# Order of the softmax steps and of the rotary products in the latent attention of a diffusion backbone step

## What is computed

```
q_nope, q_rope = mla_queries(...)          # rmsnorm(x @ w_dq) @ w_uq, 8 heads of 128 + 64
q_rope = rope_2d(q_rope)                   # latent tokens only
k_nope = (ckv @ w_uk).reshape(b, nk, 8, 128)
v = (ckv @ w_uv).reshape(b, nk, 8, 128)
s = (einsum('bqhd,bkhd->bhqk', q_nope, k_nope)
     + einsum('bqhr,bkr->bhqk', q_rope, k_rope)) * MLA_SCALE
p = softmax(s, axis=-1)
o = einsum('bhqk,bkhd->bqhd', p, v)
out = o.reshape(b, -1, 1024) @ w_o
```

## Time and profile before

| What | us |
|---|---|
| Median of three runs | 3872.28 |
| Profiled execution | 3875.15 |
| its span on the core | 3873.3 |
| TensorE matmuls, busy in the span | 3490.6 (90%) |
| VectorE busy | 2095.7 (54%) |
| ScalarE busy | 1322.9 (34%) |
| GpSimd busy | 1294.9 (33%) |
| Mean granted clock of TensorE | 0.957 |
| Key products with the four swaps | 3108.22 to 3130.79 |
| Value products | 3130.79 to 3149.6 |
| Loop over the items with the last value product | 3150.3 to 3316.0 |

### The profile page before, as it was taken

The page is one execution under the profiler, slowest core; times in us unless marked ns, Lnnn a source line. Parts: engine busy times, 40 slices in busy tenths (PEclk is TensorE's granted clock), DMA queues, the critical chain, the costliest instruction groups (busy, mean ns, idle before and its releaser), DMA issues.

```text
span 3873.3 us, 67086 instructions
## 1 busy us (share of the span) xinstructions
PE 3490.6 (90%) x24914; PEld 3232.6 (83%) x24914; DVE 2095.7 (54%) x3521; ACT 1322.9 (34%) x2244; POOL 1294.9 (33%) x577
## 2 busy tenths in 40 slices
PE   4899999999999988983699999999998698999998
PEld 2689999898899977962588888889997576789997
DVE  8553674564356558388676766435654554341113
ACT  2253224414422254374233322442224223443223
POOL 0255334545533344302300000553335210454334
PEclk9999999999999999976799999999999799999999
DMA  6434554433454433466121110345443210343223
GB/s 222 137 120 148 189 195 142 120 92 115 131 179 169 149 110 117 134 207 206 51 60 53 54 58 27 123 131 177 166 151 117 63 36 1 93 126 97 74 73 116
DMA packets 173378, 457.72 MB, mean 118 GB/s; under 512 B 56784, under 2 KB 66448, under 8 KB 172432
## 3 DMA queue, kind: packets, MB, share of 16 engines
q1 hardware_dynamic: 145408, 438.46, 35.5%
q10 hardware_dynamic: 27792, 16.83, 1.4%
HBM read 416.79 MB, written 38.44 MB: 118 GB/s over the span
## 4 chain that ended last, share of the span: by engine, by line
issue 73%; POOL 15%; PE 6%; POOLq 2%; DMA 1%; ACT 1%; DVE 1%; DVEq 0%; ACTq 0%; SPq 0%
POOL ws L687 15%; PE banks L760 2%; PE banks L781 1%; PE banks L765 1%; POOLq L723 1%; POOLq L718 1%; PE banks L791 1%; POOLq L695 0%; PE banks L985 0%; PE banks L1015 0%; DMA inv_a<-blk_d 0%; PE banks L1038 0%; DMA wr<-in_w_slabs 0%; POOLq L686 0%; DMA l<-in_l 0%
## 5 line engine op out<-in xcount | busy, mean ns | idle before, releaser
L687 POOL TENSOR_TENSOR ws<-wr,ws 128x1024 fp32r<-128x1024 f32 x509 | 1239.5, 2436 | 2405.6 <-ACT ws L1453 2404.9
L1453 ACT ACTIVATE ws<-wr 128x1024 fp32r<-128x1024 f32 x509 | 538.0, 1057 | 1117.2 <-PE banks L765 441.4
L760 PE MATMUL banks<-hs,ws 128*128 128x320 f32 x3712 | 564.3, 309 | 0.4 <-DVE hs L2496 0.3
L760 PEld LDWEIGHTS banks<-hs,ws 128*128 128x128 f32 x3712 | 549.3, 188 | 1.2 <-DVE hs L2496 0.9
L781 PE MATMUL banks<-hs,ws 128*128 128x320 f32 (+2 forms) x2624 | 443.2, 320 | 58.6 <-DVE hs L2141 19.6
L781 PEld LDWEIGHTS banks<-hs,ws 128*128 128x128 f32 x2624 | 404.0, 194 | 87.4 <-issue 31.7
L781 PE MATMUL banks<-fs,ws 128*128 128x320 f32 x2304 | 374.1, 314 | 20.0 <-DVE acc L2862 11.3
L781 PEld LDWEIGHTS banks<-fs,ws 128*128 128x128 f32 x2304 | 347.2, 190 | 37.8 <-issue 13.8
L2294 DVE SCALAR_TENSOR_TENSOR mjunk<-mr,banks 128x1024 f32<-128x1024 f32 x284 | 335.6, 1219 | 73.6 <-DMA mr<-in_m_slabs 48.5
L760 PE MATMUL banks<-fs,ws 128*128 128x320 f32 x2304 | 351.7, 310 | 0.0
L760 PEld LDWEIGHTS banks<-fs,ws 128*128 128x128 f32 x2304 | 342.3, 189 | 2.4 <-issue 2.4
(11 more groups left out here) (308 smaller groups left out, 4528.1 us busy)
## 6 DMA issues: line engine op xcount, KB each, us to landing
wr<-in_w_slabs SPq DMA_DIRECT2D x509, 512.0 KB, 3.6
mr<-in_m_slabs SPq DMA_DIRECT2D x167, 512.0 KB, 5.0
ar_d<-ar SPq DMA_DIRECT2D x16, 640.0 KB, 4.0
bk_d<-bt SPq DMA_DIRECT2D x16, 640.0 KB, 5.2
ar<-ar_d SPq DMA_DIRECT2D x16, 640.0 KB, 4.2
bk<-bk_d SPq DMA_DIRECT2D x16, 640.0 KB, 5.4
mx<-in_m_slabs SPq DMA_DIRECT2D x16, 512.0 KB, 6.6
rkv<-rkv_d SPq DMA_DIRECT2D x24, 320.0 KB, 4.8
```

The source lines that it names most:

```text
L687: pool.tensor_tensor(ws[s % 2][:, 1, :], wr[:, s % 2, :], ws[s % 2][:, 0, :].bitcast(F32), ALU.subtract).then_inc(lo_ready, 1)
L760: pe.matmul(pu[:, t % 2, h, 0:HT], ws[s % 2][:, 0, k * P:(k + 1) * P], src[:, k, part, h * HT:(h + 1) * HT], start=(k + part == 0), stop=F ...
L1453: act.activation(ws[s % 2][:, 0, :], wr[:, s % 2, :], ACT.Copy).then_inc(hi_ready, 1)
```

## The change

It has two parts. On VectorE the loop over the items now does `maximum(n + 1)` ahead of `normalise(n)` rather than behind it. And the four swaps on TensorE and the four rotations on VectorE, which stood between the key products, now stand together ahead of them. No instruction is added or removed.

```diff
@@ TensorE, latent_attention @@
                         product(j, NQ, j * QR, lambda k: hs[:, k], slab[0])
                     slab[0] += 1
+                for j in range(MH // 2):
+                    swapped(1 + j, qr[:, j, 0:LAT], t_q + MH + j + 1)
                 pe.wait_ge(h_ready, h_tiles[0] + NQ + NKV)
...
                     for j in range(4):
                         product(j, NKV, j * KVR, lambda k: hs[:, NQ + k], s)
-                        if j % 2:
-                            i = 2 * b + j // 2
-                            swapped(1 + i, qr[:, i, 0:LAT], t_q + MH + i + 1)
                     slab[0] += 1
@@ VectorE, latent_attention @@
                     take_tile(qr[:, j, :])
                 dve.drain()
+                for j in range(MH // 2):
+                    rotate(1 + j, qr[:, j, 0:LAT])
                 for b in range(2):
...
                     for j in range(4):
                         take_tile(kn[:, 4 * b + j, 0:T])
-                        if j % 2:
-                            i = 2 * b + j // 2
-                            rotate(1 + i, qr[:, i, 0:LAT])
...
                 for n in range(n_items):
-                    normalise(n)
                     if n + 1 < n_items:
                         maximum(n + 1)
+                    normalise(n)
                     if n % 5 == 1 and n > 5:
                         take_values(n // 5 - 1)
```

## The result

The changed kernel takes 3990.22 us (median of three, 3989.37 to 3991.47) against 3872.28: the ratio is 1.0303, with a 95% interval of 1.0280 to 1.0326. The forecast was 3941 with a range up to 3975; the direction was right, the size was not. The loss is 118 us where 69 were forecast. The rival with the bad clock (3973) came nearest and was still short.

The account below looks back on a forecast made before the run. TensorE was taken to nearly fill the attention loop, so time comes from what makes it wait. Loop stalls +51.4, clock +12 and rotations +5.8 sum to 69.2 us: 3944.4 profiled, forecast 3941 us, range 3918 to 3975.

Parts of the forecast that it names:

- The rival with the bad clock: Attention loop: TensorE's clock swings as in the worse row, mean 0.74, costing 44 us; 3973 us, chance 0.13.
- The stall: Attention loop: each turn waits for VectorE's reduce, multiply, reciprocal and scaling behind the scores, 1.96 us per latent item.
- The net of all turns: Attention loop: new stalls of 70.8 us less present ones of 19.4, net +51.4 us, bounds +45 and +55.
- a mean of 0.90, nearer the milder row: Attention loop: TensorE's mean granted clock falls from 0.97 to 0.90, 46 us slow rather than 10, costing +12 us.
- the upper end of 44: Attention loop: clock cost if its mean were 0.74, with half the time slow, +44 us.
- the upper bound of every term, 55 + 44 + 8: Bounds: loop stalls with slower semaphore hops +55, loop clock at 0.74 +44, swaps and rotations +8 us.
- The two rows that I compared: Profile windows near the new loop's 68% share: 13.76 busy of 20.00 us, clock 0.98, and 13.03 of 20.00, 0.74.
- the fall at 3224.70: TensorE idled 1.7 of 3.70 us before 3224.70, then ran at clock 0.55 for 3.40 us.
- +8.9 - 3.2 in the key stage: Key products start at 3117.1 rather than 3108.2 behind serial rotations, +8.9 us; swaps no longer inside save 3.2.
- -1.9 in the value stage: Value products no longer meet a rotation that is late beside GpSimd, whose wait was 1.93: -1.9 us.
- clock +2: Swap stretch: TensorE does about 3 us of work in 8 us, so the lower clock is expected, +2 us.
- this part's bound of -2: Swaps and rotations: -2 us if the products could start after the second swap and no clock fell.

Follow-up runs that it names:

- before_fill: Kernel before the change, plus two matmuls of 384 columns that nobody reads between the context scores and the turn behind them: 3872.8 us, ratio 0.9999.
- late_turn: Maximum ahead of normalise, but TensorE's turn and ScalarE's copy one item later, swaps and rotations as before the change: 3873.42 us, ratio 0.9998 to the kernel before.
- context_only: Kernel before the change, with maximum ahead of normalise only where the next item is the context one, 8 of 39 places: 3873.56 us, ratio 0.9999.
- softmax_only: Kernel before the change with only the exchange of maximum and normalise, swaps and rotations left between the key products: 3979.0 us, ratio 1.0265.
- softmax_fill: Only the exchange of maximum and normalise, plus two matmuls of 384 columns that nobody reads ahead of each turn: 3924.22 us, ratio 1.0133 to the kernel before.
- rotary_only: Kernel before the change with only the swaps and rotations moved ahead of the key products, loop order kept: 3887.39 us, ratio 1.0034.
- late_turn_fill: Maximum first and the turn one item later, plus two matmuls that nobody reads behind the context scores: 3867.8 us beside 3871.26 for the kernel before, ratio 0.9992.

## Why the prediction was wrong

**The mechanism and the waits: right.** The stall was worked out at 1.96 us for a latent item; the rows show 2.04 of weight-load idle less 0.12, so 1.92. The net of all turns was put at 51.4 us and came out at 51.7 by the waits, 52.7 against before_fill. late_turn, which keeps the exchange and loses nothing, shows that the cost comes from the place where the turn stands; context_only shows none where the scores end early.

**The clock: the step that failed.** "I take a mean of 0.90, nearer the milder row", +12 us. The mean was 0.70 (0.72 in softmax_only) and the cost 59 us, five times the term, and beyond even the upper end of 44 that I had taken from the row at 0.74. The way from the mean to the cost was right: with 0.70 in its place 0.6 x 277 = 166 us are slow rather than 10, TensorE works in 75% of them, and half of that is lost, 59 us. Only the mean was wrong, and it falls outside the 0.74 to 0.98 beyond which the prediction called itself wrong. With the upper bound of every term, 55 + 44 + 8, the forecast would have been 3979 us, still 11 short. Two things led to the mean. The two rows that I compared had the right busy share over 20 us, but a mean over 20 us says nothing on how the gaps lie in it; the better guide stood in the same group, the fall at 3224.70 behind 3.70 us with 1.7 of idle. That is about the mix of work and gap which the change puts into every item, and I used that row only to show that falls exist. And the gaps don't go away when the clock is low: the turns wait 1.85 us for VectorE at either level, and the clock comes back and falls again. A stretch of the changed loop:

```profile
3212.00:3219.00 7.00, 4.71 (x20) 0.74 0.00 0
```

Taken in windows of 1 us, its clock is 1.00 from 3214 to 3216, 0.50 from 3217 to 3223, 1.00 again from 3224 to 3226 and 0.50 from 3227. I had bounded the clock by rows of other stages; the bound should have reached to the case in which most of the loop runs at 1.2 GHz.

Two rules of the Trainium skill were weighed, both of its page "TensorE: Matmul & The Clock Gate". The section "A second HAM failure mode: psum-queue depth-cycling" says that frequent short idles between groups of matmuls make the clock swing; this case agrees, though its idles come from waits for VectorE (softmax_only at 0.72 against softmax_fill at 1.00). The section "HAM oscillation — how this bites in real kernels" warns only of idle gaps longer than any here; the weight loads of the turns wait at most 2.5 us, and the clock falls all the same.

**The rotations: right in kind, small in size.** Forecast +8.9 - 3.2 in the key stage, measured 6.7 at full clock; -1.9 in the value stage, measured 19.51 to 17.43, -2.1; clock +2, measured 3.6 (32.87 to 29.26). The sum was 8.2 rather than 5.8. (The low end of the range, 45 + 0 + 0, gives 3917 rather than 3918, and it left out this part's bound of -2.) The three waits for VectorE in a row are there; the first rotation met GpSimd as forecast. rotary_only's timeline at the swaps:

```profile
3115.28 2.06 DVE L2760 TENSOR_TENSOR qr<-ta,tb 128x512 f32<-128x512 f32 x1
...
3115.34 1.10 PE L1304 MATMUL banks<-qr,swap 128*128 128x512 f32 x2 [1.53 <-DVE tb L2758]
...
3118.87 1.10 PE L1304 MATMUL banks<-qr,swap 128*128 128x512 f32 x2 [2.44 <-DVE tb L2758]
...
3121.04 2.04 PE L1304 MATMUL banks<-qr,swap 128*128 128x512 f32 x2 [1.07 <-DVE tb L2758]
```

What stays open: why the exact mean was 0.70 and not, say, 0.80. The runs show that it lies in TensorE's gaps and that one idle matmul per item, about 0.65 us of work, removes nearly all of it; they don't show a law for it.

## What to carry to other kernels

When an operation moves ahead of another on one engine, look at what the engine that is waited for has queued between the two: here the maximum waits for scores that TensorE does right before the turn, so cover of 2.57 us turned into a stall of 1.92. When a change puts gaps of that size into TensorE's stream, price the clock as a term of its own. Here it cost as much as the gaps (59 us beside 52) with 1.9 us in each item, and nearly nothing once one filler had cut them to about 1.3 (1.92 less 0.65), so no fixed ratio carries over. Take it from the stretch of the trace whose gaps lie like the new ones, not from one with the same mean. Idle matmuls in such a gap are a cheap test of how much is clock, and here won back 55 us of 104.

## What was not expected of the hardware

A gap of about 1.9 us behind each 3.06 us of TensorE's work (its length at full clock) brought the granted clock of a whole stage to 0.70 and 0.72, and one idle matmul of about 0.65 us in each gap brought it back to 0.98. Also, the loop that is best in its own stage (156.8 us rather than 165.7) moved the median of the run by 3.5 us only. In their traces the loops of before_fill and late_turn_fill are shorter by 4.3 and 8.9 us, and the ratios of 11 runs each allow at most 3.9 and 6.6 us. The stages behind the loop don't take the gain back: they last 557.5 and 557.4 us in these traces and 557.3 before. The loops of the executions without a trace are not known, so it stays open where the rest went; runs of one kernel spread over some 13 us here (3865.83 to 3879.17 for the kernel before in one series).
